# Mixer-to-experts hand-over of a one-core diffusion step: normed rows on VectorE, a sixth weight slot, earlier expert numbers, shares reordered on chip

## What is computed

```
h = rmsnorm(x, norm1) * (1 + scale1) + shift1
x = x + gate1 * mixer(h)                       # short conv branch and latent attention branch
h = rmsnorm(x, norm2) * (1 + scale2) + shift2
x = x + gate2 * hier_moe(h)
y = rmsnorm(x, final_norm)
# hier_moe: softmax over 4 groups, best group; softmax over its 8 experts, best 2 per token;
#   share a of expert e = p_group * p_e / (sum of the two)
#   out = sum over the two experts of share * (silu(h @ w_gate[e]) * (h @ w_up[e])) @ w_down[e]
```

## Time and profile before

| | |
|---|---|
| median of 3 runs | 974.52 us (971.74 to 976.48) |
| the profiled execution: its time | 976.25 us |
| its span from first to last instruction | 974.3 us |
| busy share of the span | PE 91%, DVE 42%, ACT 28%, POOL 12% |
| bytes moved | 198.84 MB, mean 204 GB/s |
| chain that ended last | PE 71%, DMA 12%, SP queue 7%, DVE 5%, ACT 4% |

### The profile page before, as it was taken

One profiled execution on the slowest core, in us unless ns is written; L12 is line 12 of the kernel. 1 busy time (PEld: TensorE's weight loads), 2 busy tenths in 40 slices (PEclk: granted clock), 3 DMA queues, 4 the chain that ended last, 5 costly groups with the idle time before them and its releaser, 6 DMA issues.

```text
span 974.3 us, 14903 instructions
## 1 busy us (share of the span) xinstructions
PE 884.4 (91%) x6001; PEld 693.6 (71%) x6001; DVE 407.5 (42%) x845; ACT 275.3 (28%) x500; POOL 116.1 (12%) x121
## 2 busy tenths in 40 slices
PE   3698888999989999999999999993999999898886
PEld 3487546888789999999999997872555555454441
DVE  1537335444425343352423193468333444343332
ACT  5334835454420312112022132332111111111122
POOL 0000000000000000000000040032233323222220
PEclk9899998999999999999999999996899999999999
DMA  9951583102212212221231134759999999999928
GB/s 346 366 207 54 207 314 99 59 33 68 67 51 87 77 53 86 86 67 63 86 148 44 47 130 110 222 171 360 407 361 411 415 408 415 406 406 410 397 95 324
DMA packets 84451, 198.84 MB, mean 204 GB/s; under 512 B 12034, under 2 KB 43772, under 8 KB 84268
## 3 DMA queue, kind: packets, MB, share of 16 engines
q1 hardware_dynamic: 77292, 184.34, 51.9%
q0 software_dynamic: 7104, 13.74, 3.8%
HBM read 189.31 MB, written 18.17 MB: 213 GB/s over the span
## 4 chain that ended last, share of the span: by engine, by line
PE 71%; DMA 12%; SPq 7%; DVE 5%; ACT 4%; issue 1%; DVEq 0%; POOLq 0%; ACTq 0%
PE pair L1228 11%; PE pair L1230 11%; PE pair L1232 11%; PE pair L760 8%; DMA w_ug<-in_w_gate 6%; PE pair L1221 5%; PE pair L1222 5%; PE pair L1223 5%; PE pair L779 4%; SPq L473 4%; PE pair L1368 3%; SPq L477 2%; PE pair L1390 2%; PE pair L1380 2%; DMA ada_b<-in_w_ada 2%; PE pair L748 2%
## 5 line engine op out<-in xcount | busy, mean ns | idle before, releaser
L760 PE MATMUL pair<-w_ug,xgT 128*64 128x256 f32 x1184 | 142.8, 396 | 14.8 <-DMA w_ug<-in_w_gate 13.5
L1560 ACT CAST hi<-raw 128x2048 fp32r<-128x2048 f32 (+3 forms) x36 | 63.3, 1758 | 231.4 <-PE pair L1232 202.0
L1737 DVE TENSOR_TENSOR lo<-raw,hi 128x2048 fp32r<-128x2048 f32 (+3 forms) x36 | 78.6, 2182 | 118.5 <-ACT hi L1560 118.0
L760 PEld LDWEIGHTS pair<-w_ug,xgT 128*64 128x64 f32 x1184 | 85.7, 142 | 58.6 <-DMA w_ug<-in_w_gate 12.0
L1228 PE MATMUL pair<-hT,hi 128*128 128x320 f32 x512 | 116.8, 309 | 0.0
L1230 PE MATMUL pair<-hT,hi 128*128 128x320 f32 x512 | 116.7, 309 | 0.0
L1232 PE MATMUL pair<-hT,lo 128*128 128x320 f32 x512 | 116.5, 309 | 0.0
L1230 PEld LDWEIGHTS pair<-hT,hi 128*128 128x128 f32 x512 | 85.7, 188 | 0.0
L1232 PEld LDWEIGHTS pair<-hT,lo 128*128 128x128 f32 x512 | 85.7, 188 | 0.0
L1228 PEld LDWEIGHTS pair<-hT,hi 128*128 128x128 f32 x512 | 85.4, 188 | 0.2 <-issue 0.2
L894 ACT ACTIVATE sa<-pair 64x256 f32<-64x256 f32 x37 | 14.1, 381 | 210.6 <-PE pair L760 210.6
(11 more groups left out here) (316 smaller groups left out, 1406.5 us busy)
## 6 DMA issues: line engine op xcount, KB each, us to landing
w_ug<-in_w_up SPq DMA_DIRECT2D x32, 1024.0 KB
w_ug<-in_w_gate SPq DMA_DIRECT2D x32, 1024.0 KB
w_dn<-in_w_down SPq DMA_DIRECT2D x32, 1024.0 KB
raw<-in_w_in SPq DMA_DIRECT2D x20, 1024.0 KB, 5.3
ada_a<-in_w_ada SPq DMA_DIRECT2D x16, 1024.0 KB, 9.4
ada_b<-in_w_ada SPq DMA_DIRECT2D x8, 1024.0 KB, 11.0
ya<-expert_rows SPq DMA_DIRECT2D x5, 1024.0 KB, 9.1
raw<-in_w_conv_out SPq DMA_DIRECT2D x4, 1024.0 KB, 5.3
```

The costliest lines, as they stand in the source:

```text
L760: x = pe.matmul(bank[2 + d % 2][g * SL:(g + 1) * SL, 0:DE], xgT[d % 2][:, k, h * SL:(h + 1) * SL], w_ug[r][:, g, h, k, :], start=(n == 0), ...
L1560: act.copy(hi[n % 2][:, 0:size], raw[n % 4][:, 0:size]).then_inc(hi_done, 1)
L1737: dve.tensor_sub(lo[n % 2][:, 0:size], raw[n % 4][:, 0:size], hi[n % 2][:, 0:size].bitcast(F32)).then_inc(lo_done, 1)
```

## The change

- The five normed rows are made by DVE alone, in two steps: `row_gain` (x * gain2, as soon as the block of x is there) and `row_shift` (times r, plus shift2). There are four buffers. POOL only issues the stores.
- `RING` is 6. The memory of the mixer is laid out anew (halves of `hT`, order of `hi` and `lo`), so that slots 2 and 3 of `w_ug` are free behind the third piece of the last product. Down slots 3 and 5 lie over the router's scratch tables.
- `rows_b[:, 0:NE]` and its product come directly behind `rank`, and `expert_i[0:32]` is copied before the tables. The first four lists come ahead of the spill arithmetic.
- SP issues in another order (in the diff). gate2 is loaded behind the weights of places 4 and 5. The number of extra tiles (`extra_of`) is read behind the last of the 30 places, no longer ahead of place 4.
- The shares are reordered by two products of PE with a doubled identity, and two operations of DVE, in turns 3 and 4. The DRAM tensor is gone.

```diff
-RING = 5
+RING = 6
@@ sp_moe
-        def rows_out(i):
-            sp.wait_ge(s_h2, i + 1)
-            sp.dma_start(H2D[i * P:(i + 1) * P, :], h2p[i % 2][:, :]).then_inc(h2_w[i % 2], 16)
-        for i in range(NT - 1):
-            rows_out(i)
-        sp.wait_ge(piece_used, N_MIX + 4)
-        load_ug(2, 2)
+        sp.wait_ge(piece_used, N_MIX + 3)
+        for p in range(2, PRE):
+            load_ug(p, p)
         sp.wait_ge(s_mixe, 2 * NT)
         load_down(0, 0)
-        rows_out(NT - 1)
-        for st in range(2):
-            for h in range(2):
-                sp.dma_start(gate2[h * SL:(h + 1) * SL, st, :].rearrange("p (g c) -> p g c", g=2),
...
-        sp.wait_ge(s_lg, NT)
-        load_down(1, 1)
-        load_ug(3, 3)
-        for p in range(2, PRE):
-            load_down(p, p)
-        X = extra_of(sp)
+        sp.wait_ge(s_h2g, NT)
+        sp.wait_ge(s_lg, NT)
+        for p in range(1, PRE - 1):
+            load_down(p, p)
+        sp.wait_ge(s_extra, RANKED)
+        ex4 = ranked(PRE)
+        load_ug(ex4, 4)
+        ex5 = ranked(PRE + 1)
+        load_ug(ex5, 5)
+        rows_stored(sp)
+        for st in range(2):
+            for h in range(2):
+                sp.dma_start(gate2[h * SL:(h + 1) * SL, st, :].rearrange("p (g c) -> p g c", g=2),
...
+        load_down(ex4, 4)
+        ex6 = ranked(PRE + 2)
+        sp.wait_ge(s_ug, LAST[0] + 1)
+        load_ug(ex6, 0)
+        sp.wait_ge(s_rdy, 3)
+        load_down(3, 3)
+        load_down(ex5, 5)
+        sp.wait_ge(s_dn, LAST[0] + 1)
+        load_down(ex6, 0)
...
-            if p == PRE + 3:
-                sp.wait_ge(s_exp_in, 3)
-                sp.dma_start(SHD.rearrange("(i p) a -> p i a", p=P), share[:, :, :]).then_inc(s_shm, 16)
-            if p == PRE + 5:
-                sp.wait_ge(s_shm, 16)
-                sp.dma_start(share_r[:, :], SHD.rearrange("(g t) a -> g (t a)", t=SL)).then_inc(s_shm, 16)
@@ pool_moe
-            pool.tensor_add(h2p[i % 2][:, :], h2s[i % 2][:, :], shift2[:, stream[i], :]).then_inc(s_h2, 1)
+            rows_out(i)
@@ dve_moe, behind rank
+        dve.tensor_scalar(rows_b[:, 0:NE], iota[0:NE, :], rank, None, ALU.is_equal).then_inc(s_route, 1)
+        dve.wait_ge(s_route_ps, FIRST_PS)
+        link(dve.tensor_scalar(r_l[:, 0:PRE], bank[7][:, 128:128 + PRE], cst[:, K_HALF:K_HALF + 1], None, ALU.add))
+        dve.tensor_add(lists[:, 0, 0:PRE], bank[7][:, 128 + PRE:128 + 2 * PRE], r_l[:, 0:PRE]).then_inc(s_rdy, 1)
...
+        dve.wait_ge(s_route_ps, NUMBERS)
+        dve.tensor_copy(expert_i[0:1, 0:NE], bank[6][0:1, 64:64 + NE]).then_inc(s_extra, 1)
@@ the rows on DVE
+        def row_gain(i):
+            dve.wait_ge(s_mixe, NT + i + 1)
+            link(dve.tensor_mul(h2_rows[i % 4][:, :], x1[:, i, :], gain2[:, stream[i], :]))
+        def row_shift(i):
+            dve.wait_ge(s_rms2, i + 1)
+            link(dve.reciprocal(stat[:, 64 + i:65 + i], stat[:, R2 + 8 + i:R2 + 9 + i]))
+            dve.scalar_tensor_tensor(out=h2_rows[i % 4][:, :], in0=h2_rows[i % 4][:, :], scalar=stat[:, 64 + i:65 + i],
+                                     in1=shift2[:, stream[i], :], op0=ALU.mult, op1=ALU.add).then_inc(s_h2g, 1)
```

More of the change, by code:

```diff
@@ L131, in constants @@
     c[:, K_PAIR:K_PAIR + SL] = np.repeat(np.eye(SL), 2, axis=0)
+    for a in range(2):
+        c[a::2, K_PAR + a] = 1
     c[0:NE, K_COL] = np.arange(NE)
@@ L257, in build @@
     actT = [sb(f"actT{i}", [P, 2, SL]) for i in range(2)]
+    gate2 = sb("gate2", [P, 2, HD])
     mixed = sb("mixed", [P, 2 * NT, SL])
[L259 to L265, removed]
@@ L276, in build @@
[L276 to L284, removed]
+    behind_rows = sb("behind_rows", [P, P])
+    assert sum(placed) >= p6_bytes
+    first_table = len(placed)
+    router = ExitStack()
@@ new lines, in build @@
+    lx_b = sb("lx_b", [NE, 1], BF16, scope=router)
+    tab_b = sb("tab_b", [NE, 2], BF16, scope=router)
+    rows_b = sb("rows_b", [NE, EXT + X_MAX // 2 + 1], BF16, scope=router)
+    mask = sb("mask", [P, NT, NE], BF16, scope=router)
+    r_t = sb("r_t", [P, 2, NT, NE], scope=router)
+    r_gs, r_ge, r_gh = (sb(f"r_g{i}", [P, NT, NG], scope=router) for i in range(3))
+    r5 = [sb(f"r5_{i}", [P, NT], scope=router) for i in range(8)]
+    r10 = [sb(f"r10_{i}", [P, 2, NT], scope=router) for i in range(5)]
@@ L285, in build @@
+    r_k = sb("r_k", [P, 2 * NT, NM], scope=router)
+    r_x = [sb(f"r_x{i}", [NE, NE + 1], scope=router) for i in range(3)]
+    r_c = [sb(f"r_c{i}", [NE, 1], scope=router) for i in range(9)]
+    r_l = sb("r_l", [P, TILES], scope=router)
+    r_v = sb("r_v", [P, TILES], scope=router)
+    router.close()
+    del placed[first_table:]
+    dn_over = [sb(f"w_dn{i}", [P, 2, D]) for i in (3, 5)]
+    behind_router = sb("behind_router", [P, (6 * PIECE * 4 - sum(placed)) // 4])
     ug_late = [sb(f"w_ug{i}", [P, 2, 2, 4, DE]) for i in range(2, 4)]
-    dn_late = [sb(f"w_dn{i}", [P, 2, D]) for i in range(2, 4)]
@@ L287, in build @@
-    spare = sb("spare", [P, (RINGS - sum(placed) + 31) // 32 * 8])
+    dn_late = sb("w_dn2", [P, 2, D])
+    ug_late.append(sb("w_ug5", [P, 2, 2, 4, DE]))
     assert sum(placed) >= RINGS
@@ L296, in build @@
     p7 = ExitStack()
-    w_ug = [sb(f"w_ug{i}", [P, 2, 2, 4, DE], scope=p7) for i in range(2)] + ug_late
+    w_ug = [sb(f"w_ug{i}", [P, 2, 2, 4, DE], scope=p7) for i in range(2)] + ug_late[0:2]
     early = ExitStack()
@@ L616, in step @@
                 scatter(j0, d - 2)
+        pool.wait_ge(s_xg0, 2)
+        rows_stored(pool)
         pool.wait_ge(s_rdy, 1)
-        for i in range(2):
-            pool.wait_ge(h2_w[i], 16 * (3 - i))
-        pool.wait_ge(s_xg0, 2)
         for d in range(2):
@@ L722, in pe_moe @@
         list_sums(0, 128, PRE, first_val)
+        pe.wait_ge(s_route, RANKS)
+        pe.matmul(bank[6][0:1, 64:64 + NE], col_b[0:NE, 0:1], rows_b[:, 0:NE], start=True, stop=True
+                  ).then_inc(s_route_ps, 1)
         pe.wait_ge(s_route, SPILL)
@@ L742, in full_lists, with share_rows @@
             list_sums(1, 0, TILES, tile_val)
+        def share_rows():
+            pe.wait_ge(s_exp_in, 3)
+            pe.wait_ge(s_pairTe, 1)
+            for h in range(2):
+                x = pe.matmul(bank[7][:, 2 * NT * h:2 * NT * (h + 1)],
+                              sq2[:, h * P:(h + 1) * P],
+                              share[:, :, :].rearrange("p i a -> p (i a)"), start=True, stop=True)
+            x.then_inc(s_pairT, 1)
         def turn(j0, d):
@@ L790, in step @@
             act_turn(j0, d)
+            if isinstance(j0, int) and d == 3:
+                share_rows()
         turn(0, 0)
@@ L1168, in _ @@
             sp.wait_ge(gm_w[i], 16 * (N_CHUNK // 2))
-        sp.dma_start(sgm[:, :, :], GMD).then_inc(s_sgm, 16)
+        for kh in range(2):
+            sp.dma_start(sgm_half[kh][:, :, :], GMD[:, 4 * kh:4 * kh + 4, :]).then_inc(s_sgm, 16)
         for mp in range(4):
@@ L1287, in _ @@
                 for i in range(NT):
-                    x = prod(bank[i][:, 0:LAT], [t[:, kk, i * P:(i + 1) * P] for t in hT],
+                    x = prod(bank[i][:, 0:LAT], [hT(t, kk)[:, i * P:(i + 1) * P] for t in range(2)],
                              [t[:, k, :] for t in wv], kk == 0, kk == KD - 1)
@@ L2023, in _ @@
                                       op0=ALU.add, op1=ALU.mult))
-        scale_rows(0)
-        for i in range(1, NT - 1):
-            add_y(1, i)
-            scale_rows(i)
+        add_y(1, 1)
+        row_gain(0)
+        row_shift(0)
+        add_y(1, 2)
+        row_gain(1)
+        row_shift(1)
+        add_y(1, 3)
+        row_gain(2)
+        row_shift(2)
+        row_gain(3)
         add_y(1, NT - 1)
-        dve.wait_ge(s_lgT, 2)
-        lg_rows(0)
-        lg_rows(1)
+        row_shift(3)
+        row_gain(4)
         dve.wait_ge(s_lgT, 4)
-        lg_rows(2)
-        lg_rows(3)
-        scale_rows(NT - 1)
+        for i in range(NT - 1):
+            lg_rows(i)
+        row_shift(4)
         dve.wait_ge(s_lgT, NT)
```

157 lines of the change are left out of this document (87 added, 70 removed).

## The result

The kernel after takes 970.25 us (median of 13 runs, 965.99 to 973.21), the kernel before in the same rounds 975.35 us (13 runs, 971.74 to 978.29). The ratio is 0.9942 (0.9927 to 0.9958): 5.6 us less, where 9.2 were forecast. The median of 970.25 lies inside the forecast's range (960.5 to 971.5) and 0.65 us above 969.6, the line under which the prediction called it faster. The profiled execution took 970.25 us, 6.0 less than the one before.

What follows compares the result with a forecast made beforehand. The prediction took the expert stage to be bound by its DMA bytes. Early weights 6.5 plus shares 3.0 made 9.5, less 0.3 for sundries 9.2 us, taking the median of 974.52 to 965.3 us; range 960.5 to 971.5.

Steps and rivals of the forecast that it cites:

- The bound: Expert stage: bound by its bytes; the end moves with the last weights' landing, and the work behind it stays the same.
- Early weights: Start of the full DMA stretch: experts 2 and 3 and place 4 issued earlier gain 6.5 us, bounds 3.5 to 8.5.
- I take 2.3: gate2's load in the full stretch: costs 2.3 us, between 1.3 for its bytes and 2.1 us more.
- Shares: Dip at 715 to 725 us: the store of 640 8-byte pieces loses 3.0 us, bounds 0 and 3.6.
- Sixth slot: Weight ring: one more slot brings nothing by itself but keeps the engines from running dry; priced at 0.
- numbers early: Routing: experts' numbers known at 672.4 instead of 677.6 us, so place 4 goes out at 673.2 instead of 679.24.
- (b): Routing: numbers come no earlier, place 4 at 678, 4.8 of the 6.5 us gone, 970.1 us; chance 0.13.
- (a): 715 to 725 us: the dip is not the shares' doing, 6.2 us gained, 968.3 us; chance 0.12.
- (c): Uneven DMA engines at the end: the dry stretch near 670 levels them, 3 to 4 us more, 962; chance 0.12.
- (d): SP stands waiting for the lists behind late gate2 in front of an empty queue: slower, say 980 us; chance 0.04.
- (e): Weight ring: stalls on slots with weights further ahead, gain given back by 745 us: 974 us; chance 0.05.

Runs made afterwards that it cites:

- The second pair: Kernel before and kernel after profiled again without edits on one chip: 974.09 us and 971.8 us, ratio 0.9964.
- the shares alone: Kernel before with only the shares reordered by two products and two operations instead of through DRAM: 973.09 us, 0.9978 of before.
- gate2 first: Kernel after with gate2's four loads issued ahead of the wait for the experts' numbers: 967.95 us, 0.9927 of before.

## Why the prediction was nearly right

**The bound.** Right. In all fourteen profiles the chain's end goes through a load of gate weights, issued some 20 us ahead, that lands just before the last up product. What comes behind that landing is the same work, as the prediction had it, but not the same time: 39.2 to 42.2 us. It is 39.2 to 39.3 in the four profiles whose last up product took 3.67 us (granted clock 1.00 in 925 to 935) and 42.2 where it took 6.54 (0.69).

**Early weights, 6.5 us.** The issues came as worked out; the term did not. The ledger gives 2.5 MB or 6.1 us at 680, and 3.4 us at 715, just under the lower bound of 3.5: 3.1 us short of 6.5. The larger part is the step "I take 2.3" for gate2, 1.0 us above its bytes, with the end at 2.1 above them: the stretch 680 to 715 loses 1.09 MB, 2.7 us. The rest was missing at 680 already, 6.1 us where the 6.5 and the 1.0 that gate2 had yet to cost make 7.5. Part of it is the start: place 4 left 0.8 us late, and the 0.85 us for its first byte, an estimate that no row gave, was too little, as the engines were full only from 676, 2.0 us behind the issue. The upper end came from the shortfall of the earlier trace rows, where gate2 followed one expert's up and gate weights and one down load; right behind the up and gate weights of two experts, all issued within 3 us, the same four loads take 11.8 us instead of 6.5, most of it behind the weights ahead of them (the prediction had 10.3 us for these), and then go with a rate of 283 GB/s. What a load costs the others was read at one place of the queue and carried to another.

**Shares, 3.0 us.** Right: alone 2.1 us (0.4 to 4.0), by the rate 1.2 MB or 2.9 us. The fixed overhead a packet of the Trainium skill (DMA: Bandwidth & Descriptors, "Why small descriptors are slow"), from which the prediction worked out 0.2 us, does not account for these 640 pieces of 8 bytes in a full queue; the measurement decides.

**Sixth slot, 0, and numbers early.** Both right: the slot's cover is worth 1.7 to 3.8 us, which it doesn't add but keeps. That the numbers' delay turns into time nearly one for one was rival (b)'s price, and holds: 3.72 us later, 2.7 to 4.9 us more.

**What no term had: the layout.** "The memory of the mixer is laid out anew" was costed at nothing. It moved the four slots at multiples of 256 away from them, and the rate in 725 to 825 went from 413 to 406 GB/s; 32 bytes do the same to the kernel before and cost 2.8 us. The account of the profiled executions: 6.5 becomes 3.4, 3.0 becomes 2.9, and the rate takes 1.7 in 725 to 825 and 0.7 in 825 to 900 (403 GB/s for 407), which leaves 3.9 us against 4.5 measured at the last landing. The second pair, by the same ledger from 600 us on, gives 2.2 against 1.4. So the account holds to within 1 us in each pair. That the time came out inside the range is in part luck: the layout's 2.4 us stood in no term, and only a range wide enough for other things took them in.

**The rivals.** (a), the dip not the shares', fell with the shares alone. (b) did not occur: numbers at 673.02. (c), engines that end level, brought nothing to be seen: 929.07 is later than the 924 of the forecast. (d) happened in its mechanism, not in its size: gate2, `gate_mul`, the lists and SP hang together as written, but 5.3 us of longer landing, not 14, and SP came back at 695.36, close to the 695.7 at which the prediction had the issued work run out; the share in 690 to 695 was still 0.99. (e) was kept off by the sixth slot.

**Open.** Why the 1 KB pieces move at 168 GB/s in the kernel after and at 351 in the kernel before, among larger ones, was not tried. The ledger has gate2 first 2.1 MB or 5.2 us ahead of the kernel after at 715, and its medians only 1.5 to 3.6 us. In its profile the last gate weights do land 6.2 us earlier (922.85), but 2.5 of these are the earlier entry, which is the execution's and not the edit's; that execution also took 965.76 us, 2.2 under its median.

## What to carry to other kernels

Where bytes are the bound, keep a ledger of bytes per stretch: a lead that is won early has to survive each later stretch, and small pieces (8 bytes, 1 KB) belong in a pause of the queue, not behind megabytes of weights. A new memory layout is an edit with a price of its own: compare where the large buffers start, and start the rows of a stream at multiples of 256 bytes. Between single profiles, compare where each enters the stage before reading a landing as the edit's. A DMA share of 1.03 says nothing of the rate: 406 and 418 GB/s show the same share.

## What the runs showed of the hardware

- Loads of weights (rows of 4 KB in each partition) move 406 to 407 GB/s into buffers that start 32, 192 or 224 bytes past a multiple of 256, and 415 to 418 GB/s where all start at a multiple. The Trainium skill (DMA: Bandwidth & Descriptors, "How a descriptor splits into AXI transactions") says that a transfer is cut at 256-byte boundaries and that one not starting there pays for the bytes ahead of it. It says so of what a transaction reads; here the starts are those of the buffers written. By it a row of 4096 bytes takes 135 beats of 32 bytes instead of 128 at a start of 224, an estimated 5%, but only 129 at a start of 32, an estimated 0.8%. The runs agree in the sign; the size they show is 2 to 3%, also in the kernel with starts of 32 and 224.
- Four loads of 128 KB in pieces of 1 KB took 6.5 us each (median) to land when the last of some 3 MB of weights had been issued 5 us ahead, and 11.8 us right behind 4.2 MB; 685 to 690 us then moved 283 GB/s in one execution of the kernel after and 252 in the other.
- A store of 640 pieces of 8 bytes costs a full queue 1.2 MB of weights, though it is 5 KB.
- A 20-column DVE operation took 2.04 us while POOL added a block of 1024 columns, and 0.18 us in the kernel after, where POOL computed nothing then (662.03 us).
